# First up tile of every MLP multiplied with the tokens stationary, one half of the tokens after the other

## The reference

```python
def _rmsnorm(x, g):
    y = x * lax.rsqrt(jnp.mean(x * x, axis=-1, keepdims=True) + RMS_EPS)
    return y * g

def _sq_relu_mlp(h, w_up, w_down):          # h (256, 1024), w_up (1024, 4096)
    u = jax.nn.relu(h @ w_up)
    return (u * u) @ w_down                  # w_down (4096, 1024)

# layers 0 and 1
x = x + mixer(_rmsnorm(x, norm_mix[i]))
x = x + _sq_relu_mlp(_rmsnorm(x, norm_ffn[i]), mlp_w_up[i], mlp_w_down[i])
# layers 2 and 3
x = _layer_norm(ALPHA * x + mixer(x), ...)
x = _layer_norm(ALPHA * x + _sq_relu_mlp(x, w1, w2), ...)
```

## Time and profile before

| | us |
|---|---|
| median of 3 runs | 1516.95 (1516.81 to 1517.58) |
| the profiled execution | 1518.57 |
| its span in the profile | 1516.8 |
| PE busy (matmuls) | 1409.6 (93%) |
| DVE busy | 913.9 (60%) |
| ACT busy | 675.4 (45%) |
| granted clock of PE, mean | 0.972 |

### The profile page before, as it was taken

One profiled execution on the slowest core, in us unless ns is written; L12 is line 12 of the kernel. 1 busy time (PEld: TensorE's weight loads), 2 busy tenths in 40 slices (PEclk: granted clock), 3 DMA queues, 4 the chain that ended last, 5 costly groups with the idle time before them and its releaser, 6 DMA issues.

```text
span 1516.8 us, 26931 instructions
## 1 busy us (share of the span) xinstructions
PE 1409.6 (93%) x11772; PEld 1233.9 (81%) x11782; DVE 913.9 (60%) x1448; ACT 675.4 (45%) x1145; POOL 72.0 (5%) x69
## 2 busy tenths in 40 slices
PE   6889999999789999999997987999999997899997
PEld 5877999988657899987897985799997974599996
DVE  6686555671485556555966434765557459855556
ACT  5844544552363445441821222354444445354452
POOL 0004000000141000000001310000000000000000
PEclk9989999999889999999999999999999999999999
DMA  7334554552301555453150000455545440245451
GB/s 306 138 123 155 197 192 175 207 183 87 142 1 56 182 189 200 167 192 130 67 189 37 4 3 30 158 190 177 212 167 190 173 166 1 102 160 210 167 195 55
DMA packets 16917, 215.17 MB, mean 142 GB/s; under 512 B 1896, under 2 KB 1936, under 8 KB 3872
## 3 DMA queue, kind: packets, MB, share of 16 engines
q1 hardware_dynamic: 15168, 205.51, 37.0%
q0 software_dynamic: 1632, 7.94, 1.5%
HBM read 212.38 MB, written 1.06 MB: 141 GB/s over the span
## 4 chain that ended last, share of the span: by engine, by line
PE 76%; DVE 16%; ACT 4%; issue 2%; DMA 1%; POOL 0%; SPq 0%; DVEq 0%
PE psum L561 21%; PE psum L441 11%; PE psum L442 11%; PE psum L443 11%; PE psum L862 5%; DVE w_low L1484 5%; PE psum L962 2%; PE psum L508 2%; PE psum L491 2%; PE psum L510 2%; PE psum L509 2%; ACT w_high L1078 2%; PE psum L456 1%; PE psum L417 1%; DVE x L1531 1%
## 5 line engine op out<-in xcount | busy, mean ns | idle before, releaser
L1484 DVE TENSOR_TENSOR w_low<-ring,w_high 128x1024 fp32r<-128x1024 f32 x368 | 437.2, 1227 | 251.7 <-ACT w_high L1078 251.7
L1078 ACT ACTIVATE w_high<-ring 128x1024 fp32r<-128x1024 f32 x368 | 368.0, 1046 | 173.3 <-PE psum L561 154.6
L441 PE MATMUL psum<-act_split,w_high 128*128 128x256 f32 x1472 | 425.0, 289 | 3.6 <-DVE w_low L1484 3.5
L442 PE MATMUL psum<-act_split,w_high 128*128 128x256 f32 x1472 | 418.3, 284 | 0.0
L443 PE MATMUL psum<-act_split,w_low 128*128 128x256 f32 x1472 | 418.0, 284 | 0.0
L441 PEld LDWEIGHTS psum<-act_split,w_high 128*128 128x128 f32 x1472 | 284.0, 193 | 9.7 <-issue 4.4
L561 PE MATMUL psum<-w_high,up_split 128*128 128x512 f32 x1024 | 287.3, 391 | 0.8 <-DVE up_split L1587 0.8
L442 PEld LDWEIGHTS psum<-act_split,w_high 128*128 128x128 f32 x1472 | 284.3, 193 | 1.3
L443 PEld LDWEIGHTS psum<-act_split,w_low 128*128 128x128 f32 x1472 | 284.2, 193 | 0.0
L561 PEld LDWEIGHTS psum<-w_high,up_split 128*128 128x128 f32 x1024 | 191.0, 189 | 40.4 <-issue 2.4
L561 PE MATMUL psum<-w_low,up_split 128*128 128x512 f32 x512 | 163.5, 390 | 0.0
(11 more groups left out here) (293 smaller groups left out, 1455.3 us busy)
## 6 DMA issues: line engine op xcount, KB each, us to landing
ring<-weights SPq DMA_DIRECT2D x96, 2048.0 KB, 8.1
work<-rows POOLq DMA_DIRECT2D x4, 1024.0 KB, 6.5
work<-rows POOLq DMA_DIRECT2D x4, 512.0 KB, 5.7
con<-consts SPq DMA_DIRECT2D x1, 1088.0 KB, 8.7
x<-x_in SPq DMA_DIRECT2D x2, 512.0 KB, 4.5
work<-t_bias POOLq DMA_DIRECT2D x1, 1024.0 KB, 10.1
out<-x SPq DMA_DIRECT2D x4, 256.0 KB, 2.0
work<-rows SPq DMA_DIRECT2D x1, 512.0 KB, 6.1
```

Source lines behind the costliest of these rows:

```text
L441: mm(out, w_hi, x_hi, start=start, stop=False)
L442: mm(out, w_hi, x_lo, start=False, stop=False)
L1078: A(high[:, HIGH_SLOT[name], f], ring[:, n % RING, f], ACT.Copy).then_inc(weights_high, 1)
L1484: V.tensor_tensor(low[:, n % RING, f], ring[:, n % RING, f], high[:, HIGH_SLOT[name], f].bitcast(f32), ALU.subtract).then_inc(weights_spli ...
```

## The change

In all four MLPs the first block (b = 0) is done in another way; blocks 1 to 7 stay as they are.

- The up tile goes through `project_tokens`: stationary are 128 tokens of `act_split`, moving are 512 columns of weights. 2 halves x 8 chunks x 3 = 48 matmuls of 512 columns. Its first half asks only for the activations of half 0. The transposes of half 1 (`norm(i, 1)`) stand in it, after chunks 5 and 6 of half 0, and the 14 + 6 matmuls on zeros become 2 ahead of the tile.
- Hidden values now have the tokens on the partitions. ReLU and square are done on 128 x 512 (one per half), and the squares are transposed by PE (4 transposes of 128 x 128 per half, `first_transposes`). Those of half 0 stand after chunk 4 of half 1, those of half 1 after piece m = 1 of the down tile's half 0. ACT then takes the high part from PSUM and DVE the low part (128 x 512 each, one per half).
- The down tile of block 0 runs half by half: 24 matmuls of half 0, then 24 of half 1.
- ACT and DVE split all four quarters of the down tile ahead of the first ReLU and the first square. The next up tile is split in two pairs of quarters round the high and low part of half 1.
- The `norm(i, 1, 14)` calls go, `mlp(layer, 6)` becomes `mlp(layer, 2)`, and the counts of `up_squared`, `up_split` and `up_high` leave block 0 out.

```diff
@@ tensor, mlp
+                def first_transposes(th):
+                    q = first + 1 + 2 * th
+                    open_bank(q)
+                    pe.wait_ge(sig("first_squared"), 2 * layer + th + 1)
+                    for m in range(4):
+                        last = nc.tensor.transpose(bank(q)[:, P * m:P * m + P], up_sq_tokens[:, th, P * m:P * m + P],
+                                                   cst("ident"))
+                    last.then_inc(bank_filled, 1)
+
+                def first_ready(th, k):
+                    if k % 4 == 0:
+                        read_out(pe, TR[i][(th, k // 4)])
+
+                def first_beside(th, k):
+                    at = k - 5
+                    if th == 0 and at in (0, 1):
+                        norm(i, 1, halves=(at,))
+                    if (th, k) == (1, 4):
+                        first_transposes(0)
+
+                open_bank(first)
+                idle(first, warm)
+                project_tokens(f"up{layer}_0", [first, first + 2], act_split, first_ready, first_beside)
                 for b in range(FBLOCKS):
...
-                    for m in range(4):
+                    for m in range(4 if b else 0):
...
+                    if b == 0:
+                        for th in range(2):
+                            read_out(pe, first + 1 + 2 * th)
+                            for m in range(4):
+                                if th == 0:
+                                    quarter_in(name, m)
+                                for a, w in ((0, w_hi), (0, w_lo), (1, w_hi)):
+                                    for n in range(2):
+                                        last = down(m, th, n, [(a, w)], m == 0 and a == 0 and w is w_hi, False)
+                                if (th, m) == (0, 1):
+                                    first_transposes(1)
+                        last.then_inc(sig("down_done"), 1)
@@ tensor, behind each project_out
-            norm(1, 1, 14)
-            mlp(0, 6)
+            mlp(0, 2)
@@ scalar, mlp
+                def first_relu(th):
+                    q = TURN[("up", layer, 0)] + 2 * th
+                    filled(q)
+                    taken(A(up_relu_tokens[:, th, :], bank(q), ACT.Relu), q)
+
+                def first_high(th):
+                    q = TURN[("up", layer, 0)] + 1 + 2 * th
+                    filled(q)
+                    done(A(up_split[:, :, 0, P * th:P * th + P], bank2(q, 4), ACT.Copy), "first_high")
+
+                split(f"down{layer}_0")
+                first_relu(0)
+                first_high(0)
+                first_relu(1)
+                split(f"up{layer}_1", [0, 1])
+                first_high(1)
+                split(f"up{layer}_1", [2, 3])
+                for b in range(1, FBLOCKS):
@@ vector, mlp
+                def first_square(th):
+                    read_out(dve, TURN[("up", layer, 0)] + 2 * th)
+                    r = up_relu_tokens[:, th, :]
+                    done(V.tensor_tensor(up_sq_tokens[:, th, :], r, r, ALU.mult), "first_squared")
+
+                def first_low(th):
...
+                split(f"down{layer}_0")
+                first_square(0)
+                first_low(0)
+                first_square(1)
+                split(f"up{layer}_1", [0, 1])
+                first_low(1)
+                split(f"up{layer}_1", [2, 3])
+                for b in range(1, FBLOCKS):
```

More of the change, by code:

```diff
@@ L340, in tile_done @@
                 layer, b = name[2:].split("_")
-                eng.wait_ge(bank_filled, TURN[("up", int(layer), int(b))] + 4)
+                eng.wait_ge(bank_filled, TURN[("up", int(layer), int(b))] + (4 if int(b) else 3))
             elif name[0:4] == "down":
@@ L536, in mlp @@
                     open_bank(acc[half])
+                i = 2 * layer + 1
+                first = TURN[("up", layer, 0)]
+                def first_transposes(th):
[18 more added lines that the diff above has]
+                project_tokens(f"up{layer}_0", [first, first + 2], act_split, first_ready, first_beside)
                 for b in range(FBLOCKS):
                     name = f"up{layer}_{b}"
-                    w_hi, w_lo = split_tile(name)
-                    for m in range(4):
+                    if b:
+                        w_hi, w_lo = split_tile(name)
+                    for m in range(4 if b else 0):
                         q = TURN[("up", layer, b)] + m
                         open_bank(q)
-                        if b == 0 and m == 0:
-                            idle(q, warm)
                         for k in range(NC):
@@ L564, in down @@
                         return last
-                    if b < FBLOCKS - 1:
+                    if b == 0:
[10 more added lines that the diff above has]
+                        last.then_inc(sig("down_done"), 1)
+                    elif b < FBLOCKS - 1:
                         for m in range(4):
                             quarter_in(name, m)
-                            pe.wait_ge(sig("up_split"), 4 * FBLOCKS * layer + 4 * b + m + 1)
+                            pe.wait_ge(sig("up_split"), 4 * (FBLOCKS - 1) * layer + 4 * (b - 1) + m + 1)
                             for th in range(2):
@@ L572, in mlp @@
                                     for n in range(2):
-                                        last = down(m, th, n, [(a, w)], b == 0 and m == 0 and a == 0 and w is w_hi,
-                                                    False)
+                                        last = down(m, th, n, [(a, w)], False, False)
                         last.then_inc(sig("down_done"), 1)
@@ L1054, in _ @@
             project_out("da_o", 7, act_split, first_half(o_in))
-            norm(7, 1, 14)
-            mlp(3, 6)
+            mlp(3, 2)
         @block.scalar
@@ L1146, in mlp @@
                         taken(A(up_relu[:, m, :], bank(q, T), ACT.Relu), q)
-                        act.wait_ge(sig("up_squared"), 4 * FBLOCKS * layer + 4 * b + m + 1)
+                        act.wait_ge(sig("up_squared"), 4 * (FBLOCKS - 1) * layer + 4 * (b - 1) + m + 1)
                         A(up_split[:, m, 0, :], up_sq[:, m, :], ACT.Copy).then_inc(sig("up_high"), 1)
@@ L1577, in mlp @@
             def mlp(layer, next_tile):
-                for b in range(FBLOCKS):
+                def first_square(th):
[3 more added lines that the diff above has]
+                def first_low(th):
+                    q = TURN[("up", layer, 0)] + 1 + 2 * th
+                    dve.wait_ge(sig("first_high"), 2 * layer + th + 1)
+                    t = slice(P * th, P * th + P)
+                    taken(V.tensor_tensor(up_split[:, :, 1, t], bank2(q, 4), up_split[:, :, 0, t].bitcast(f32),
+                                          ALU.subtract), q)
+                split(f"down{layer}_0")
[6 more added lines that the diff above has]
+                for b in range(1, FBLOCKS):
                     for m in range(4):
@@ L1581, in mlp @@
                         q = TURN[("up", layer, b)] + m
-                        at = 4 * FBLOCKS * layer + 4 * b + m + 1
+                        at = 4 * (FBLOCKS - 1) * layer + 4 * (b - 1) + m + 1
                         read_out(dve, q)
```

11 lines of the change are left out of this document (4 added, 7 removed).

## The result

The changed kernel takes 1518.75 us (median of 20 runs, 1517.76 to 1523.97), the kernel before 1517.03 (20 runs). The ratio is 1.0014 with a 95% interval of 1.0008 to 1.002: 2.1 us slower (1.2 to 3.0); the two medians alone differ by 1.7. Forecast were +4.0 us (1521.0) and a range of 1514.8 to 1525.0. The direction is as forecast. A later set of 11 runs of the changed kernel gave 1.0016 (1.0007 to 1.0025). Each set of runs has its own runs of the kernel before beside it (medians 1517.03, 1518.09 and 1517.66), so kernels of different sets are compared by their ratios.

The account below looks back on a forecast made before the run. PE was taken as the bound, busy for 93% of the span. The form and overlap gave -2.0 us, four slow-clock stretches +6.0, so +4.0 on the median 1516.95: 1521.0 us, range 1514.8 to 1525.0.

Parts of the forecast that it names:

- A stall of 3.1 us for the first square: Block 0's up tile, half 1: PE waits 3.1 us for DVE's square, which stands behind four quarters of the split.
- The recorded sum: Layer 2: DVE's quarters end at 986.88, the square of about 0.69 follows, and PE goes on at 987.65.
- Each stall brings one slow stretch: Behind each of four waits, 3.41 us at half clock, priced at 1.5 us each, 6.0 us in all; chance 0.62.
- The prediction's bound from the earlier trace: PE's clock: a wait of 1.66 us is followed by a half-clock stretch, one of 1.52 us is not.
- The sum without the clock, -2.0 us: Four MLP starts: 1.24 us gained in each of two layers, 0.24 us lost in each of the other two.
- layer 2's clock: Layer 2's step times, moved 850.06 us ahead for layer 0, put block 1 there at 151.46 against 151.22, 0.24 us lost.
- Mixers and blocks 1 to 7 shift as a whole: Outside the changed blocks: durations stay the same, 0 us with 0.5 us either way.
- The clock did not hold: Rival for the four waits: full clock stays although PE waits, time 1515.0 us; chance 0.15.
- It did not fall at the tile's start either: Rival: the clock falls at the up tile's start too, up to four more stretches, 1527.4 us, two 1524.2; chance 0.12.
- the first square comes in time: Rival: the first square is there when PE asks at 984.56, without waits or slow stretches, -14.4 us, 1502.6; chance 0.08.

Follow-up runs that it names:

- the early square: The changed kernel, but ACT and DVE split only one quarter of the down tile ahead of the first ReLU and square: 1504.48 us, ratio to before 0.9909.
- POOL held back: The changed kernel with POOL's 16 operations in layer 0 waiting until block 1's up tile is done: 1519.46 us, ratio 1.0014.
- the zeros in the wait: The changed kernel with 13 matmuls on zeros ahead of the transposes of the first half's squares: 1517.21 us, ratio 0.9995.
- the delayed kernel: The kernel before with 18 in place of 6 matmuls on zeros ahead of layer 0's up tile: 1518.91 us, ratio 1.0007; again, one run, 1518.65 us.

## Why the prediction was right, and where it was off

1. **A stall of 3.1 us for the first square.** Right in place, cause and size: 2.85 to 2.86 us of idle in layers 1 to 3. It is shown by the early square, which removes it by order alone. The recorded sum has a slip: 986.88 + 0.69 + 0.17 is 987.74 and not 987.65. The measured 987.63 is nearer to the slip, since the square started at 986.80.
2. **Each stall brings one slow stretch.** Right: four of four, in each of the four profiles of this form with the wait (POOL held back among them). Its price was set a little low: 1.5 forecast, 1.7 measured with the zeros in the wait. The Trainium skill ("TensorE: Matmul & The Clock Gate", "Why this matters for your kernels") warns of long idle gaps of PE, behind which it comes back at half its clock; this trace agrees, with 0.50 behind all sixteen waits of 2.85 to 3.68 us in the MLP starts. The prediction's bound from the earlier trace rows doesn't stand, though: it rests on one wait on each side. In the twelve profiles here, 18 waits of 1.65 and 1.66 us in the sparse attention began at full clock; a stretch at 0.50 followed 9 of them and not the other 9. The wait of 2.9 us at the end of layer 2's MLP brought one in eleven profiles and not in the twelfth, the first of the delayed kernel, where the clock stays at 1.00 behind a wait of 2.93 us (from 1165.34). So a stretch behind each of four waits was likely and not certain.
3. **The sum without the clock, -2.0 us.** With the zeros in the wait the stages give -1.4: +1.01, +0.19, -1.32, -1.24, against +0.24, +0.24, -1.24, -1.24 forecast. Three of four are right to 0.1 us. The fourth, layer 0, is a step that failed: I carried layer 2's clock over to it ("everything behind it runs on the same clock"). DVE is slower there, as POOL works from 127.98 on; the kernel before has POOL's 16 operations at the same place (from 128.15).
4. **"Mixers and blocks 1 to 7 shift as a whole", 0 with 0.5 us either way.** Right for the blocks (0.05 us). Wrong for the mixers: -5.0 us in the profile, some -3.5 by the runs. This is why +5.6 in the stages were +2.1 in the runs, and why the forecast of +4.0 was too high though its own terms were too low. The terms were 1.6 us short and the mixers gave more than that back; that the total still came within 2 us is luck in part. In the delayed kernel the length of the attention mixer goes with the place of the slow stretches, with the same instructions. The RWKV mixer follows the same pattern (17.1 us at half clock in the changed kernel, 23.9 before, 27.3 to 34.1 in the profiles where it was longer), but no kernel of its own was tried on it. Why the three profiles of the changed kernel have their stretches at the same places stays open.
5. **The rivals.** The clock did not hold. It did not fall at the tile's start either, with the wait of 1.20 to 1.35 us there, the transposes ahead of it and only two matmuls on zeros: no stretch in any profile. That the first square comes in time was priced at -14.4 us; once the order allowed it, the stages gave -13.7.

The mean over executions stays partly open. There is one profile of the kernel before, and how often which set of stretches occurs, these profiles don't tell.

## What to carry to other kernels

When a consumer is moved forward, list what its producer's queue does ahead of the value and move that too: the overlap was worth 14 us here, and four quarters of a split ahead of one square ate it all. A wait of PE of 2.9 us cost 1.7 us more than itself by the clock, so either fill it or remove it. A difference of a few us is read stage by stage: stages that nobody changed moved by -4 to +5 us here, and one of them by 2.1 us between two profiles of one kernel, while the changed stages repeated to 0.3 us.

## What the runs showed of the hardware

- DVE is slowed by POOL's work: 128 x 1024 subtractions took 1.41 us beside POOL's tensor_scalar and 1.23 without (4 quarters 5.23 and 4.63), a square of 128 x 512 0.88 and 0.68 to 0.69.
- Behind the waits of PE of 2.85 to 3.68 us in the MLP starts the granted clock was 0.50 for 3.41 us, in 16 of 16; between dense matmuls such a stretch cost 1.67 to 1.82 us. Behind 1.65 to 1.66 us of idle it was 0.50 in 9 of 18 cases. Matmuls on zeros in the wait kept it at 1.00, in 4 of 4.
- The same instructions of a mixer took from 4.0 us less to 0.04 us more (sparse attention) and from 2.5 less to 4.7 more (RWKV) than in the profile of the kernel before, with the stretches at 1.2 GHz in other places. One kernel, run twice, differed by 2.1 us in the attention mixer.
- The transposes in a row of matmuls cost little: 4 of 128 x 128 take 0.35 us from start to start (978.90 to 979.25), and the matmuls behind them 0.1 more.
